# First stage of a two-block transformer layer pair: vectors loaded by SyncE, norm weights issued first, four x tiles turned into own PSUM banks, the meta tile turned after the first weight unit

## The reference

```python
h = jnp.concatenate([lead, meta, x], axis=1)
...
a = rmsnorm(h, g_mix[layer])
proj = jnp.einsum('bld,de->ble', a, w_in[layer])
sb_q, sb_k, sb_v, hg_q, hg_f, hg_i, hg_g = jnp.split(proj, split_idx, axis=-1)
```

## Time and profile before

| | us |
|---|---|
| median of 3 runs | 2378.21 |
| lowest, highest | 2378.13, 2389.55 |
| the profiled execution's own time | 2376.62 |
| its span, first to last instruction | 2374.8 |
| TensorE busy | 2083.6 (88%) |
| VectorE busy | 1415.8 (60%) |
| ScalarE busy | 1085.1 (46%) |
| mean granted TensorE clock | 0.925 |

### The profile page before, as it was taken

How to read it: one execution, slowest core, us unless ns; L and a number is a source line. 1 busy time by engine, 2 the same in 40 slices (tenths; PEclk the granted TensorE clock), 3 DMA queues, 4 the chain that set the end, 5 groups by cost and what they waited for, 6 DMA issues and landing times. The chain is left out here.

```text
span 2374.8 us, 25271 instructions
## 1 busy us (share of the span) xinstructions
PE 2083.6 (88%) x10228; PEld 1664.6 (70%) x10228; DVE 1415.8 (60%) x1560; ACT 1085.1 (46%) x1232; POOL 185.7 (8%) x132
## 2 busy tenths in 40 slices
PE   5999965766999999993889999997698987999997
PEld 4887655664666666662778888886577866888786
DVE  4112788357998898885159888887643345333213
ACT  4233632216888888874235544444242224222212
POOL 0001031001222222210000000000000000000000
PEclk9999888857999999996789999998899998999999
DMA  4220000406999999984133333313122222333231
GB/s 144 83 72 1 1 1 21 169 36 238 403 406 402 403 405 399 402 344 156 40 107 89 89 89 93 104 54 107 37 88 89 89 86 65 98 97 92 85 107 53
DMA packets 202060, 346.86 MB, mean 146 GB/s; under 512 B 13871, under 2 KB 149543, under 8 KB 184535
## 3 DMA queue, kind: packets, MB, share of 16 engines
q1 hardware_dynamic: 191280, 332.49, 39.8%
q0 software_dynamic: 5120, 8.40, 1.1%
q10 hardware_dynamic: 5543, 4.34, 0.6%
HBM read 340.93 MB, written 12.65 MB: 149 GB/s over the span
## 5 line engine op out<-in xcount | busy, mean ns | idle before, releaser
L1465 DVE TENSOR_TENSOR wlo_e<-raw_e,whi_e 128x2048 fp32r<-128x2048 f32 x192 | 436.4, 2288 | 57.9 <-ACT whi_e L1387 57.2
L1387 ACT CAST whi_e<-raw_e 128x2048 fp32r<-128x2048 f32 x192 | 366.7, 1912 | 72.9 <-PE pall L1548 32.1
L1768 DVE TENSOR_TENSOR w_lo<-w_raw,w_hi 128x2048 fp32r<-128x2048 f32 x89 | 203.8, 2289 | 321.1 <-ACT w_hi L1760 321.1
L48 PE MATMUL pall<-hT_hi,w_lo 128*128 128x512 f32 x864 | 347.9, 403 | 23.1 <-DVE xbc L2312 10.3
L1760 ACT CAST w_hi<-w_raw 128x2048 fp32r<-128x2048 f32 x89 | 169.4, 1904 | 428.9 <-PE pall L50 414.6
L49 PE MATMUL pall<-hT_lo,w_hi 128*128 128x512 f32 x864 | 341.9, 396 | 0.0
L50 PE MATMUL pall<-hT_hi,w_hi 128*128 128x512 f32 x864 | 341.4, 395 | 0.0
L1547 PE MATMUL pall<-whi_e,xs 128*128 128x512 f32 x512 | 208.9, 408 | 10.1 <-DVE xs L1471 5.2
L48 PEld LDWEIGHTS pall<-hT_hi,w_lo 128*128 128x128 f32 x864 | 166.0, 192 | 60.0 <-DVE xbc L2312 10.6
L1548 PE MATMUL pall<-wlo_e,xs 128*64 128x512 f32 x512 | 204.9, 400 | 0.0
L49 PEld LDWEIGHTS pall<-hT_lo,w_hi 128*128 128x128 f32 x864 | 166.0, 192 | 35.0 <-issue 0.5
(11 more groups left out here) (495 smaller groups left out, 3941.2 us busy)
## 6 DMA issues: line engine op xcount, KB each, us to landing
raw_e<-in_w_expert_up_dram SPq DMA_DIRECT2D x64, 1024.0 KB, 11.2
raw_e<-in_w_expert_down_dram SPq DMA_DIRECT2D x64, 1024.0 KB, 11.8
raw_e<-in_w_expert_gate_dram SPq DMA_DIRECT2D x64, 1024.0 KB, 11.7
w_raw<-in_w_in_dram SPq DMA_DIRECT2D x80, 512.0 KB, 5.9
w_raw<-in_w_gate_up_dram SPq DMA_DIRECT2D x44, 512.0 KB, 5.1
w_raw<-in_w_down_dram SPq DMA_DIRECT2D x22, 512.0 KB, 4.1
mixed<-in_w_in_dram SPq DMA_DIRECT2D x10, 1024.0 KB, 5.0
A<-acs_rows SPq DMA_DIRECT2D x8, 1024.0 KB, 4.8
```

Source lines behind the costliest of these rows:

```text
L48: nc.tensor.matmul(out, w_lo, m_hi, start=start, stop=False)
L1387: nc.scalar.copy(whi[j][:, :], raw[j][:, :]).then_inc(sem_hi, 1)
L1465: nc.vector.tensor_tensor(wlo[j][:, :], raw[j][:, :], whi[j][:, :].bitcast(F32), ALU.subtract).then_inc(sem_lo, 1)
L1768: (engine or self.nc.vector).tensor_tensor(self.lo[i][:, :], self.raw[i][:, :], self.hi[i][:, :].bitcast(F32), ALU.subtract).then_inc(self ...
```

## The change

- The norm weights are the first thing that ScalarE does; then it loads the activation table that has the root, and only then waits for the meta tile's zeros and issues the load of the meta tokens.
- The 14 loads of vectors go from ScalarE's queue to SyncE's, behind the third weight unit.
- `turn_banks`: tile 0 is turned into banks 6 and 7, tile 1 into 0 and 1, tile 2 into 2 and 3, tile 3 into 4 and 5, the meta tile into 6 and 7. TensorE no longer waits for low parts between tiles 0 to 3.
- The meta tile is normalised after the first two weight units' low parts, and turned between unit 0 and unit 1, ahead of the vectors. Unit 0 waits for eight low halves instead of ten, and unit 2 for ten.
- The order on ScalarE and VectorE is written out anew.

```diff
             @block.sync
...
                     sp.dma_start(dst, src).then_inc(s_raw[u % 3], 16)
+                    if u == 2:
+                        for t, tile in enumerate(VEC_TILES):
+                            at = 0
+                            for name, rows in tile:
+                                sp.dma_start(vrow[at:at + rows, t, :], srcs[name]).then_inc(s["vec"], 16)
+                                at += rows
...
             def _(act):
+                act.dma_start(gbc, dram["g_mix"][0].partition_broadcast(P)).then_inc(s["gbc"], 16)
+                nc.scalar.preload_act_table_set("sqrt_and_others")
                 act.wait_ge(s["hm0"], 1)
                 act.dma_start(hm[0:META, :], dram["meta_tokens"]).then_inc(s["meta"], 16)
-                act.dma_start(gbc, dram["g_mix"][0].partition_broadcast(P)).then_inc(s["gbc"], 16)
...
+                act.wait_ge(s["eps"], 1)
+                root(0, 0)
+                root(1, 1)
+                root(2, 2)
+                upper(0, 0)
+                root(3, 3)
+                upper(1, 1)
+                upper(2, 2)
+                upper(3, 3)
+                make_hi(0)
+                make_hi(1)
+                root(4, NT)
...
                     if u == 0:
+                        upper(4, NT)
                         act.wait_ge(s["lbd"], 1)
...
+                normal(0, 0)
+                normal(1, 1)
+                normal(2, 2)
+                lower(0, 0)
+                normal(3, 3)
+                lower(1, 1)
+                lower(2, 2)
+                lower(3, 3)
+                make_lo(0)
+                make_lo(1)
+                normal(4, NT)
+                lower(4, NT)
...
+                def turn(j, i):
                     pe.wait_ge(s["xn"], j + 1)
+                    if j == 4:
+                        pe.wait_ge(s["lo"], 2)
                     for half in range(2):
-                        if j >= 1:
-                            pe.wait_ge(s["lo"], 2 * (j - 1) + half + 1)
                         for k in range(4):
-                            last = nc.tensor.transpose(banks[6 + half][:, k * P:k * P + P],
+                            last = nc.tensor.transpose(banks[turn_banks(j) + half][:, k * P:k * P + P],
                                                        xn[j % 2][:, (4 * half + k) * P:(4 * half + k + 1) * P], ident[:, :])
                         last.then_inc(s["tr"], 1)
-                pe.wait_ge(s["lo"], 10)
+
+                for j in range(NT):
+                    turn(j, j)
+                pe.wait_ge(s["lo"], 8)
...
                     if u == 1:
+                        turn(4, NT)
                         vectors()
                     if u == 2:
                         pe.wait_ge(s["cols"], 1)
+                        pe.wait_ge(s["lo"], 10)
```

More of the change, by code:

```diff
@@ L189, in _, with root @@
             def _(act):
+                act.dma_start(gbc, dram["g_mix"][0].partition_broadcast(P)).then_inc(s["gbc"], 16)
+                nc.scalar.preload_act_table_set("sqrt_and_others")
                 act.wait_ge(s["hm0"], 1)
                 act.dma_start(hm[0:META, :], dram["meta_tokens"]).then_inc(s["meta"], 16)
-                act.dma_start(gbc, dram["g_mix"][0].partition_broadcast(P)).then_inc(s["gbc"], 16)
[L193 to L211, removed]
+                def root(j, i):
                     if i == NT:
@@ L220, in _, with make_hi, upper @@
                                          scale=1.0 / D).then_inc(s["rt"], 1)
+                def make_hi(u):
+                    act.wait_ge(s_raw[u % 3], 16 * (u // 3 + 1))
+                    if u >= 2:
+                        act.wait_ge(s["wused"], u - 1)
+                    nc.scalar.copy(whi[u % 2][:, :], raw[u % 3]).then_inc(s["whi"], 1)
+                def upper(j, i):
+                    for half in range(2):
+                        act.wait_ge(s["tr"], 2 * j + half + 1)
+                        nc.scalar.copy(aT_hi[:, 4 * half:4 * half + 4, i * P:i * P + P],
+                                       banks[turn_banks(j) + half][:, :].rearrange("p (k t) -> p k t", k=4)).then_inc(s["hi"], 1)
+                act.wait_ge(s["eps"], 1)
[10 more added lines that the diff above has]
+                root(4, NT)
                 act.wait_ge(s["never"], 2)
@@ L228, in _ @@
                                      scale=0.0)
[L229 to L247, removed]
                 def evacuate(o):
@@ L299, in lower, with normal @@
                         nc.vector.tensor_tensor(aT_lo[:, 4 * half:4 * half + 4, i * P:i * P + P],
-                                                banks[6 + half][:, :].rearrange("p (k t) -> p k t", k=4),
+                                                banks[turn_banks(j) + half][:, :].rearrange("p (k t) -> p k t", k=4),
                                                 aT_hi[:, 4 * half:4 * half + 4, i * P:i * P + P].bitcast(F32),
                                                 ALU.subtract).then_inc(s["lo"], 1)
-                dve.wait_ge(s["gbc"], 16)
-                for j, i in enumerate(TILES):
+                def normal(j, i):
                     dve.wait_ge(s["rt"], j + 1)
@@ L312, in _ @@
                                                    gbc, ALU.mult, ALU.mult).then_inc(s["xn"], 1)
-                    if j >= 1:
[L314 to L317, removed]
+                dve.wait_ge(s["gbc"], 16)
+                normal(0, 0)
[10 more added lines that the diff above has]
+                lower(4, NT)
                 dve.wait_ge(s["vtr"], 1)
```

20 lines of the change are left out of this document (18 added, 2 removed).

## The result

| | before | after |
|---|---|---|
| median, us | 2378.36 (6 runs) | 2367.74 (6 runs) |
| lowest, highest | 2373.53, 2389.55 | 2362.92, 2369.36 |
| ratio | | 0.9947, 95% interval 0.9926 to 0.9967 |
| profiled execution, its span | 2376.62, 2374.8 | 2364.32, 2362.4 |

The changed kernel is 10.6 us faster by the medians, 12.6 by the ratio and 12.4 by the two spans. The forecast said 12.65 and 2365.6. The median lies 2.1 us above that, inside the stated range of 2362 to 2371 and 0.8 above the narrower span of the forecast; the interval of the ratio leaves out 1.

A forecast was written before the change was run, and what follows sets the result against it. The serial start before TensorE's first product (35.45 us) was taken as the bound, moving everything behind it equally. First product 13.75 us sooner, 1.1 back for meta turns: -12.65, from 2378.2 to 2365.6 us; range 2362 to 2371.

The forecast's parts named there:

- the signs of being wrong: First reciprocal at 9 or later, over twenty slow products in the first unit, or later stages not moving by the same amount.
- R: When VectorE makes the first reciprocal: 10.51 us before, forecast about 7.0, bounds 6.0 and 9.0; 3.5 us of the gain.
- neither counts if the weights land last: At ScalarE's start: early table load and dropped 1.28 us second load gain nothing if the norm weights arrive last.
- The chain behind R: From first reciprocal to TensorE's first product: replayed as 14.5 us, plus 0.2 for x tile 2 landing late; product at 21.7.
- The fourteen issues: ScalarE's vector-load issues ahead of its first high half: 5.67 us of sequencer time said to stand on the path.
- Meta turns: The meta tile's eight turns between the first two units on TensorE, where it has no slack: 1.1 us given back.
- The slow opening: First unit's first twelve products at 1.2 GHz, 0.44 us each: 5.3 us slow again; range none to whole unit.
- The cover of the second unit's chain: 3.9 us of slack before the third unit's product absorbs 2.5 us of additions, cost 0; rival: cover gone, 1 to 1.5 us, 0.05.
- The line for "faster": Set at 2366.3 us, 11.9 (about 0.5%) below before; faster 0.60, within 0.5% 0.37, slower 0.03.
- Late norm weights: Rival: norm weights don't come sooner, first reciprocal at 9.0 to 9.5, gain 10.2 to 10.7 us, 2368.0; chance 0.18.
- late vectors: Rival: TensorE waits behind the meta turns for the fourteen loads; slower than before if landed after 49.0 us; chance 0.03.
- The clock as a rival: Pause before first product keeps TensorE at 1.2 GHz through unit 0, 7 us more, 2372.5, chance 0.10; or up at once, 2363, 0.07.

The follow-up runs named there:

- the second pair: The kernel before and the changed kernel each traced once more, word for word; first attention-score matmul (the hand-over, H) at 225.7 and 211.3 us, executions 2373.61 and 2360.25.
- a_gbc_old: Changed kernel with ScalarE's start as before: meta tokens' load, then norm weights', no early table load; first product 24.21 us against 21.58, execution 2369.76.
- a_gbc_sp: Changed kernel with the norm weights issued by SyncE between x tiles 0 and 1 instead of by ScalarE; first product 22.26 us against 21.58, execution 2366.19.
- a_no_preload: Changed kernel with norm weights still issued first but without the early table load; first product 23.82 us against 21.58, execution 2368.8.
- a_vec_act: Changed kernel with the fourteen vector loads back on ScalarE's queue, behind the constants; first product 21.45 us against 21.58, execution 2375.14.
- the two larger sets of runs: Both kernels unchanged, run again in one call: 17 runs of the kernel before, median 2381.3 us; 12 of the changed kernel, median 2367.83, ratio 0.9946.

## Why the prediction was right, point by point

**What bounds.** Right: the head start at the first product, 13.87, was still 13.9 at the hand-over 190 us later. Of the signs of being wrong one did appear in the first pair of traces, a later stage that moved by less (10.6 us at the last piece of scores); in the second pair it moved by 14.0, so scatter is enough to explain it.

**R, the first reciprocal.** Forecast 7.0, with 6.0 to 9.0 as bounds; measured 7.66. The norm weights came as worked out (6.3, "near 6.5"), but the term was missized at the other end: I gave the x tile a delay of 0.7 us from sharing, and it was 1.6, so that the first tile's square and root end last, not the weights. (It landed after 3.5 us in a_gbc_old and in a_gbc_sp, where the norm weights were issued later.) From that follows what the forecast got wrong in kind: "neither counts if the weights land last". a_no_preload shows that the two table loads count fully, 2.5 us between the arrival of x tile 0 and the reciprocal. I had argued the early table load away. The sum did not notice, since the changed kernel has it.

**The chain behind R.** Forecast 14.5 + 0.2; measured 21.58 - 7.66 = 13.9. Two terms differ. The second tile was late (its square at 8.51, where the replay had it ready), which also put ScalarE's first high half at 11.26 instead of near 9.8. In a_gbc_old and a_no_preload, where it was not late, the same chain took 13.65, so that cost 0.3. And then the turns ran faster than in the replay: tile 3's took 1.10 us against 1.94 before. The gain of 0.8 in the chain nearly cancels the 0.7 that R cost. So the first product stood at 21.58 against 21.7 by luck; the parts were less good.

**The fourteen issues** were the right reading of a 4.5 us wait put down to "issue" in the earlier trace rows: alone, in the old order, they were worth 4.6. The prediction put 5.67 us of ScalarE on the path; in the first 1.1 of them the four constants ran beside the issues, and they would have taken that time anyway. The rule of the Trainium skill that was weighed there (DMA: Bandwidth & Descriptors, Issuing engines are not separate DMA queues) is both borne out and limited by the runs. That transfers interleave fits the delay of x tile 0 by 1.6 us, which came only where the norm weights were issued beside it. That the choice of the queue saves only sequencer time is right as well, as a_vec_act shows; but sequencer time is small only where nothing waits behind it. Ahead of the high halves it was 4.6 us, behind them nothing.

**What comes back.** Meta turns: forecast 1.1, measured 35.13 - 34.26 = 0.87:

```profile
34.26 1.03 PE L391 MATMUL pall<-ident,xn_a 128*128 128x128 f32 x8
35.13 0.60 PE L379 MATMUL pall<-ident,vrow 128*128 128x128 f32 x4
```

The slow opening: forecast the same as before, about twelve products; measured eight at some 0.43 us (21.58 to 25.12), so unit 0 took 12.7 us and not 13.6. Together they cost nothing: at the vectors' turns the head start was 49.07 - 35.13 = 13.94, not 1.1 less than at the first product; this is the term that was off most.

The prediction took the two slow openings for the same thing, turns and then a pause, and they were not. In the kernel before every eight turns took 1.94 us, to the last at 31.55, so TensorE had not left the lower level, 1.2 GHz, when unit 0 began, only 2.0 us of waiting ahead of it. In the changed kernel it had reached the upper one with tile 3's turns and fell back in the pause of 4.9 us. The granted clock shows only the fall. For unit 0's first twelve products in the kernel before, at 0.44 us each, it says 1.00 (the last number but two):

```profile
35.40:40.70 5.30, 5.25 (x12) 4.13 (x13) 0.00 (x0) 0.00 (x0) 0.00 (x0) 1.00 0.56 194
```

So at the start of a trace, where the column stands at 1.00 from the first microsecond on, the level has to be read from the durations.

The slow opening moved between the variants too, from 12.4 us for the unit (a_gbc_old, 24.21 to 37.51 less the meta turns) to 13.8 (a_no_preload, 23.82 to 38.45 less the same), so I could have given it a range at this size, not a value. The cover of the second unit's chain held, and the fourteen loads delayed nothing: TensorE waits for nobody from its first product to H but for 0.9 us at H itself, in both kernels.

**The sum and the whole.** -12.65 was forecast, -13.9 reached the hand-over, -12.4 and -10.6 came out in spans and medians. That the spans and the ratio come within 0.3 us of the forecast is luck: the first stage gained 1.2 more than forecast, and the scatter behind it took 1.5. The line for "faster" was 11.9, and the median (10.6) and the ratio (12.6) stand on its two sides; where a program scatters by 6 to 22 us between executions, on which side of it six runs come out is partly chance, and 0.60 against 0.37 said about that. I carried the difference of 3.4 us between median and span of before over without asking what it was: 1.8 of it is what an execution takes beyond its span (2376.62 and 2374.8, and 1.9 in the changed kernel), and 1.6 is this scatter.

**The rivals.** Late norm weights, late vectors and a lost cover did not happen. The clock as a rival was right as a place and too narrow as a price: it was looked for in the first unit, where it moved 1 us, and not in the attention, where it moved 3 to 6.

## What to carry to other kernels

A DMA issue costs the engine that makes it time whether or not the transfer matters, here about 0.4 us each on ScalarE and up to 5.1 for a 1 MB weight on SyncE; look for idle time put down to "issue", and place the issues behind work that somebody waits for, which counts more than the queue they are on. Where several edits take away waits that stand beside each other, price them together: taken back singly, ScalarE's early start, own banks and the late meta tile were worth 2.6, 5.4 and 3.6 us at the first product. The queue was worth 4.6 done alone in the old order and nothing taken back in the new one, so the parts add to 16.2 or to 11.6, and not to the 13.9 that all had together. The early norm weights gave 0.4 of their 2.6 without the early table load. And where a program scatters by more than a change, compare marks in the traces: the hand-over repeated within 0.4 us, while the whole time of one program moved by 18 and 22 in the two larger sets of runs.

## What the runs showed of the hardware

Turns keep TensorE's clock up as products do: with the 4.7 us pause filled by turns of the identity, the clock stayed at 1.00 and a whole unit ran at 2.4 GHz (0.23 us a product). They also raise it: in the changed kernel the first eight turns took 1.94 us and tile 3's 1.10, before any product had run. I had not expected that the clock moves the attention of one program by 6 us between executions, with TensorE busy nearly throughout (70.25 of 72.70 and 76.42 of 78.80 us). And with a 512 KB transfer issued in the same moment on the other queue the first x tile took 5.2 us to land instead of 3.6.
